# Where the remainders' buffers lie in memory: gaps of 64 to 192 bytes between the rounded halves and the remainders of a two-block transformer kernel

## What is computed

```python
def swiglu(h, w1, w3, w2):
    return (jax.nn.silu(h @ w1) * (h @ w3)) @ w2

def moe_swiglu(h, router_w, w1, w3, w2):
    ...
    for e in range(N_EXPERTS):
        out = out + gates[..., e:e + 1] * swiglu(h, w1[e], w3[e], w2[e])
    return out

h_x = h_x + 0.5 * mx[2] * ffn1(pre(h_x, g_norm[i, 0], mx[0], mx[1]))
h_c = h_c + 0.5 * mc[2] * ffn1(pre(h_c, g_norm[i, 0], mc[0], mc[1]))
```

## Time and profile before

| | us |
|---|---|
| median of 2 runs | 2820.97 |
| lowest and highest | 2817.69 and 2824.25 |
| the profiled execution, its own time | 2821.69 |
| span of its profile | 2820.0 |

### The profile page before, as it was taken

How to read it: one execution, slowest core, us unless ns; L and a number is a source line. 1 busy time by engine, 2 the same in 40 slices (tenths; PEclk the granted TensorE clock), 3 DMA queues, 4 the chain that set the end, 5 groups by cost and what they waited for, 6 DMA issues and landing times.

```text
span 2820.0 us, 43022 instructions
## 1 busy us (share of the span) xinstructions
PE 2695.8 (96%) x17542; PEld 2432.2 (86%) x17542; DVE 1913.6 (68%) x2703; ACT 1181.7 (42%) x1510; POOL 118.1 (4%) x227
## 2 busy tenths in 40 slices
PE   3979999999999999899999999999999999999999
PEld 2879998899999999888888988888888888886999
DVE  5877678766887788777477445665666646675655
ACT  3436445454443477642132423422225223255543
POOL 0010000000000000000000000000000000000000
PEclk9989999999999999999999999999999999999999
DMA  7676766635776698745355223453544534311554
GB/s 295 222 246 229 263 233 207 241 126 178 238 238 215 231 339 310 271 143 187 137 184 170 83 89 108 152 173 114 167 146 138 170 118 164 121 60 46 178 190 142
DMA packets 116619, 511.97 MB, mean 182 GB/s; under 512 B 12608, under 2 KB 16064, under 8 KB 116304
## 3 DMA queue, kind: packets, MB, share of 16 engines
q1 hardware_dynamic: 81776, 381.92, 40.0%
q0 software_dynamic: 32112, 117.45, 12.7%
q10 hardware_dynamic: 2544, 9.96, 0.9%
HBM read 508.24 MB, written 1.05 MB: 181 GB/s over the span
## 4 chain that ended last, share of the span: by engine, by line
PE 77%; DVE 12%; ACT 4%; issue 3%; DMA 2%; ACTq 0%; DVEq 0%; POOLq 0%
PE PS L2103 22%; PE PS L2104 22%; PE PS L2105 22%; DVE wlo L1106 5%; ACT whi L579 2%; PE PS L2297 1%; PE PS L2294 1%; PE PS L2293 1%; DMA ada_first<-in_adastream 1%; DVE ada L1138 1%; PE PS L2198 1%; DMA ada<-in_adastream 1%; PE PS L2202 1%; PE PS L2199 1%; DVE PS L1138 1%
## 5 line engine op out<-in xcount | busy, mean ns | idle before, releaser
L579 ACT ACTIVATE whi<-raw 128x1408 fp32r<-128x1408 f32 (+2 forms) x540 | 717.9, 1342 | 767.9 <-PE PS L2105 709.5
L1106 DVE TENSOR_TENSOR wlo<-raw,whi 128x1408 fp32r<-128x1408 f32 (+2 forms) x540 | 840.1, 1578 | 215.2 <-ACT whi L579 214.3
L2103 PE MATMUL PS<-h_hi,whi 128*128 128x256 f32 (+1 forms) x2656 | 857.8, 323 | 19.8 <-DVE wlo L1106 13.2
L2104 PE MATMUL PS<-h_lo,whi 128*128 128x256 f32 (+1 forms) x2656 | 853.8, 321 | 0.0
L2105 PE MATMUL PS<-h_hi,wlo 128*128 128x256 f32 (+1 forms) x2656 | 853.8, 321 | 0.0
L2103 PEld LDWEIGHTS PS<-h_hi,whi 128*128 128x128 f32 x2656 | 502.2, 189 | 65.2 <-DVE wlo L1106 15.7
L2105 PEld LDWEIGHTS PS<-h_hi,wlo 128*128 128x128 f32 x2656 | 501.5, 189 | 40.1
L2104 PEld LDWEIGHTS PS<-h_lo,whi 128*128 128x128 f32 x2656 | 500.8, 189 | 39.7 <-issue 0.2
L2103 PE MATMUL PS<-hid_hi,whi 128*128 128x256 f32 (+1 forms) x1298 | 416.1, 321 | 4.6 <-DVE wlo L1106 4.6
L2105 PE MATMUL PS<-hid_hi,wlo 128*128 128x256 f32 (+1 forms) x1298 | 414.1, 319 | 0.0
L2104 PE MATMUL PS<-hid_lo,whi 128*128 128x256 f32 (+1 forms) x1298 | 414.0, 319 | 0.0
(11 more groups left out here) (464 smaller groups left out, 3229.4 us busy)
## 6 DMA issues: line engine op xcount, KB each, us to landing
raw<-in_wstream SPq DMA_DIRECT2D x243, 704.0 KB, 4.4
raw<-in_wstream SPq DMA_DIRECT2D x176, 768.0 KB, 5.7
ada<-in_adastream POOLq DMA_DIRECT2D x222, 512.0 KB, 4.5
raw<-in_wstream SPq DMA_DIRECT2D x121, 512.0 KB, 4.1
ada_first<-in_adastream ACTq DMA_DIRECT2D x6, 1536.0 KB, 22.6
X<-in_xT SPq DMA_DIRECT2D x1, 1024.0 KB, 14.1
X<-in_ctxT SPq DMA_DIRECT2D x1, 1024.0 KB, 5.5
cond<-in_c_rows POOLq DMA_DIRECT2D x1, 1024.0 KB, 6.1
```

The lines of the kernel that those rows point to most:

```text
L579: nc.scalar.activation(whi[:, (q + dp) % SLOTS, 0:n], raw[:, (q + dp) % RAW_SLOTS, 0:n], ACT.Copy).then_inc(hi_split, 1)
L1106: nc.vector.tensor_tensor(wlo[:, (q + dp) % SLOTS, 0:n], raw[:, (q + dp) % RAW_SLOTS, 0:n], whi[:, (q + dp) % SLOTS, 0:n].bitcast(F32), AL ...
L2103: mm(o, left[0], right[0], start=start, stop=False)
L2104: mm(o, left[0], right[1], start=False, stop=False)
```

## The change

Blank buffers of 64 bytes times a number, made by `gap`, take the place of the three fixed ones; where the number is 0 nothing is added. The narrow token buffers change their order: the remainder comes first. `dense_only`, a filler of the narrow set, grows by 256 bytes, as the buffers beside it do.

```diff
-        sb("line_shift", [PART, 48])
+        def gap(lines, stack):
+            gaps.append(lines)
+            return sb(f"gap{len(gaps)}", [PART, 16 * lines], F32, stack) if lines else None
...
-            sb("line_shift_both", [PART, 16], F32, s)
+            gap(0, s)
             h_hi[BOTH] = sb("h_hi", [PART, KD, BOTH], F32R, s)
+            gap(1, s)
             h_lo[BOTH] = sb("h_lo", [PART, KD, BOTH], F32R, s)
+            gap(3, s)
             with ExitStack() as s2:
+                gap(0, s2)
                 hid_hi[BOTH] = sb("hid_hi", [PART, UNITS, BOTH], F32R, s2)
+                gap(2, s2)
                 hid_lo[BOTH] = sb("hid_lo", [PART, UNITS, BOTH], F32R, s2)
             with ExitStack() as s2:
+                gap(0, s2)
                 y_hi = sb("y_hi", [PART, KD, BOTH], F32R, s2)
+                gap(3, s2)
                 y_lo = sb("y_lo", [PART, KD, BOTH], F32R, s2)
...
         with ExitStack() as s:
+            gap(0, s)
+            h_lo[SEQ] = sb("h_lo1", [PART, KD, SEQ], F32R, s)
+            gap(3, s)
             h_hi[SEQ] = sb("h_hi1", [PART, KD, SEQ], F32R, s)
-            h_lo[SEQ] = sb("h_lo1", [PART, KD, SEQ], F32R, s)
+            gap(0, s)
             with ExitStack() as s2:
+                gap(0, s2)
                 hid_hi[SEQ] = sb("hid_hi1", [PART, UNITS, SEQ], F32R, s2)
+                gap(2, s2)
                 hid_lo[SEQ] = sb("hid_lo1", [PART, UNITS, SEQ], F32R, s2)
+                gap(2, s2)
...
                 few = sb("few", [PART, UNITS * PART], F32, s2)
-                sb("line_shift_few", [PART, 32], F32, s2)
+                gap(2, s2)
                 few_hi = sb("few_hi", [PART, UNITS, PART], F32R, s2)
+                gap(1, s2)
                 few_lo = sb("few_lo", [PART, UNITS, PART], F32R, s2)
...
-                sb("dense_only", [PART, 2 * UNITS * SEQ + DENSE * SEQ], F32, s2)
+                sb("dense_only", [PART, 2 * UNITS * SEQ + DENSE * SEQ + 64], F32, s2)
```

More of the change, by code:

```diff
@@ L236, in build @@
         stage_b = sb("stage_b", [PART, 2, BOTH])
-        sb("line_shift", [PART, 48])
+        def gap(lines, stack):
+            gaps.append(lines)
+            return sb(f"gap{len(gaps)}", [PART, 16 * lines], F32, stack) if lines else None
+        gaps = []
         h_hi, h_lo, hid_hi, hid_lo = {}, {}, {}, {}
```

## The result

| | before, us | after, us |
|---|---|---|
| median of 2 runs | 2820.97 | 2858.46 |
| lowest and highest | 2817.69 and 2824.25 | 2856.57 and 2860.35 |
| the profiled execution, its own time | 2821.69 | 2860.35 |
| span of its profile | 2820.0 | 2858.7 |

The ratio is 1.0132 with a 95% interval from 1.0099 to 1.0164: the changed kernel is slower by 37.5 us. That is less than the 2% that count as a difference here, but the interval leaves 1 out. The forecast was 2815 with a range from 2790 to 2843, so the time lies 15 us above the range.

The account below looks back on a forecast made before the run. TensorE bounds it: number of passes times the interval between them, set by relative memory places. Terms 2 + 6 + 1 + 0 - 1.4 gave some 7.5 us gained, 6 after give-back: 2821 - 6 = 2815 us, range 2790 to 2843.

Parts of the forecast that it names:

- item 4: Wide 512-column passes, 1024 token and 462 unit triples: priced at 0; 3 us lost or 10 us gained considered.
- middle state: 256-column interval of 117.9 ns between fast and slow levels; assumed not to survive one different pass in three.
- Item 1: Narrow token buffers: remainder pass slow at 120 ns, both rounded-half passes fast at 113.3; 2 us gained.
- Item 2: Narrow unit buffers, 704 triples: remainder pass at 116 ns, the others at 113.3; 6 us gained.
- Item 3: 256-column halves out of the wide buffers, some 400 triples: remainder pass leaves 120 ns; 1 us gained.
- Item 5: Sparse experts, 352 triples: one load in three goes to the moving weights' place; 1.4 us lost; down passes 0.
- Item 6: VectorE and ScalarE on the moved buffers: 256-column subtraction stays at 425 ns; 0 change.
- Item 7: Latent attention's key buffers move from 128 to 192, a few dozen passes; under 1 us.
- The give-back: Waits for low weights: a faster TensorE waits longer where VectorE is late, returning 1 to 2 us.
- Rival 3: Narrow token passes: a slow remainder pass delays the next loads, making all slow; 2842 to 2847 us; chance 0.22.
- Rival 1: Restart after a wait selects fast or middle level, change only rethrows dice; 2821 us, 2812 to 2828; chance 0.24.
- Rival 2: Unlike places keep streams apart, every 256-column pass at 113.3 ns; 2788 us, or 2778 with wide passes; chance 0.18.

Follow-up runs that it names:

- uniform kernels: Six variants of the changed kernel with all moving buffers of a set at one place, so nothing steps; 2846.5 to 2866.5 us.
- lo64_pair: Changed kernel with wide remainders and low weights wlo at 0, everything else at 192; 2855.7 us, ratio 1.0136 to the kernel before.
- uni_wide64: Changed kernel with wide buffers all at 64, narrow ones at 128 as before, few at 128; 2846.5 us, ratio 1.0103 to the kernel before.
- wlo_only: All token and unit buffers at 192, only the low weights wlo moved to 0; 2852.5 us, ratio 1.0124 to the kernel before.
- lo64: Changed kernel with wide remainders at 0, everything else including low weights wlo at 192; 2868.7 us, ratio 1.0182 to the kernel before.

## Why the prediction was wrong

**What failed first: item 4, the wide passes.** It was priced at 0, "the load is over in the first half of such a pass", with 3 us lost as the bound. No row of this case showed that: the load records of the wide stretch have 188 ns each, in passes 226.7 ns apart. It was 24.1 us lost, the larger half of the result, and the text had called it the largest lever. Two things were missing. The bound came from the one row with a difference of 64 (228.9 ns), and the units' remainder lay at 64, a difference of 128, for which there was no row: by the uniform kernels its B pass costs 232.7. Pricing each pass so gives 2.2 ns by 1024 and 6.0 by 462, 5 us. The other 19 are left to the steps, which no row of before could show with 512 columns, since nothing in it stepped there.

**The assumption that carried every item** was that each pass is priced by the row with its own difference of places, and that unlike passes break the middle state in favour of the fast one. `lo64_pair` refutes the first half: differences of 0 and 231.8 ns. The second half turned out reversed in the narrow set: unlike neighbours removed the fast level.

**Item 1, narrow tokens**: 2 us gained were forecast, with 20 lost as the bound. By 1632 triples it was 9.8 ns (three times 118.35 less three times 115.1), 16 us lost, and 17.8 with the passes behind norms. The bound held, the choice within it was wrong. A and C were to become fast at 113.3; in the dense stretch A has 119.2 and C 117.0. Its B, at the weights' own place, did not stand at 120 either but at 119.2. The 348 for the triple before was also too high: mean less 163 ns gives 116, the starts give 115.1.

**Item 2, narrow units**: 6 us gained were forecast, within 8 gained and 6 lost; it was 2.2 lost, for the same reason: 117.8, and nobody fast.

**Item 3, halves out of the wide buffers**: 1 us gained forecast, 2.1 gained. Here the forecast's direction held: everything had been slow before, and with steps the passes stand near 118, below 120 and above 113. **Item 5, sparse experts**: 1.4 us lost forecast for the up passes, 0.8 measured; 1.3 for the down passes against a bound of 2. **Item 6**: VectorE's subtraction into the moved remainder has 425 ns as in the earlier trace rows:

```profile
L1226 DVE TENSOR_TENSOR h_lo<-stage_b,h_hi 128x256 fp32r<-128x256 f32 x64 | 27.2, 425 | 17.2 <-ACT stage_b L657 17.1
```

**Item 7** was not looked at by itself; the sum above closes without it. **The give-back** had the right mechanism with the other sign: the waits for low weights fell by 6 us because TensorE became slower.

**Rival 3** came nearest: slower, 2842 to 2847. Its point of decision, A and C of the dense stretch at 283, is nearly what the page shows (282 and 280 there, 285 and 281 over the span), and its mechanism, a delay that one pass leaves to the next, is what the step is. It put the cost in the narrow set alone, with 3 us for the wide one, and at the level 120; the runs put half of it in the wide set, and the narrow one at 118. **Rival 1**'s dice are real (`uni_wide64` against before), worth some 6 us for the dense stretch, but not the answer. **Rival 2**, everything at the floor, fell: every kernel with steps in its narrow set, of the moving or of the loaded tile, had 117 ns or more there.

The rule of the Trainium skill that was weighed ("SBUF — State Buffer", section "A bandwidth-pool intuition that's wrong") would have the loads of weights read through a port of their own, and the places then should not matter. In these runs the same 17,542 matmuls took from 2817 to 2869 us by addresses alone, and moving the low weights cost the wide passes of `wlo_only`, whose other places stayed, 20 us (4.2 ns by 3357 and 4.4 by 1386). The trace disagrees with the rule as it was applied. Whatever the ports are, the two streams were not independent of each other's addresses.

What is not shown: through what the two streams meet, and why 512 columns want equal places and 256 columns places 64 apart. Steps are counted here per pass and not by size, and they don't always cost: the convolution's passes (`y`, 192 against 128) have 229.0 in after, which is what their differences alone give (twice 226.7 and once 233.3 make 228.9). In `lo64` the same passes step the other way, between 192 and 0, and have 231.8, where their differences alone give 227.4. None of the layouts tried is better than the kernel before, and what selects fast or middle at a restart was not found.

## What to carry to other kernels

In this kernel the relative place of moving and loaded tile within 256 bytes was a term of every pass, and it could be priced only in the sequence in which the passes run. What to try first elsewhere: keep all moving operands at one place and all loaded tiles at one place, and then choose the difference of the two by measurement for each width (here 0 for 512 columns and 64 for 256, where no run tells which sign is better). Before a blank buffer is put in for one short kind of pass, multiply a few ns by the passes of every other kind that read those buffers; a term that is priced at 0 because something "is over by then" needs the same bound as the others. And where a level is selected by chance, compare stretches, not totals: identical addresses gave 117.9 and 113.8 ns in the same stage.

## What the runs showed of the hardware

- A pass of 512 columns took from 226.7 to 234.3 ns and one of 256 columns from 113.3 to 119.9 ns at a granted clock of 1.00, by the places of moving and loaded tile and their order; differences of -96, -32, +32 and +96 all gave 233.2 to 234.3 with 512 columns.
- Behind a change of place a pass of 512 columns takes up to 9 ns more (236 ns where both places are equal), and it takes some five passes to come back to 226.7. Between 192 and 128 no such cost was seen (229.0 in the convolution).
- With 256 columns and a difference of 64 either way there are two levels, near 113.4 and 117.8 ns, with the same addresses; at -64 each lasts for hundreds of passes, at +64 the fast one was seen for up to 106. Steps leave nothing of the fast one: the changed kernel's narrow passes stood at 117 to 119.5. The 17 us between the lowest and the highest of 13 runs of the kernel before (2809.8 and 2826.8) are of the size that this choice can make (5448 passes by 4.4 ns are 24 us), though that was not tested by itself.
